# Five turns of the gate and second output projections as seven block products, with the merge stage regrouped

## The reference

```
h = rmsnorm(x)
z = h @ w_in                     # q, k, v, the gates ga and gm, ...
a_out = forgetting_attention(...)        # 256 x 1024
m_out = rmsnorm(mlstm(...)) * sigmoid(...)   # 256 x 1024
merged = sigmoid(ga) * (a_out @ w_proj_a) + sigmoid(gm) * (m_out @ w_proj_m)
x = x + merged @ w_out           # 2048 x 2048
h2 = rmsnorm(x)
u = causal_conv(h2 @ w_up); x = x + (silu(u_gate) * u_val) @ w_down
```

## Time and profile before

| | us |
|---|---|
| median of 3 runs (2109.66 to 2109.86) | 2109.82 |
| the profiled execution's own time | 2109.87 |
| its span in the trace | 2108.1 |
| PE busy in the span | 2102.6 (100%) |
| DVE busy | 1432.9 (68%) |
| ACT busy | 1092.6 (52%) |
| POOL busy | 17.5 (1%) |

### The profile page before, as it was taken

One profiled execution on the slowest core, in us unless ns is written; L12 is line 12 of the kernel. 1 busy time (PEld: TensorE's weight loads), 2 busy tenths in 40 slices (PEclk: granted clock), 3 DMA queues, 4 the chain that ended last, 5 costly groups with the idle time before them and its releaser, 6 DMA issues.

```text
span 2108.1 us, 25121 instructions
## 1 busy us (share of the span) xinstructions
PE 2102.6 (100%) x10042; PEld 1759.9 (83%) x10042; DVE 1432.9 (68%) x1605; ACT 1092.6 (52%) x1292; POOL 17.5 (1%) x17
## 2 busy tenths in 40 slices
PE   9999999999999999999999999999999999999999
PEld 8888888888888887887888888888888888888887
DVE  7987556655787754655654555567777777779986
ACT  6765444444456544544444444555555555555553
POOL 0000000000000000000000000000000000000000
PEclk9999999999999999999999999999999999999999
DMA  8665555555764554544455555556555555556653
GB/s 335 209 203 176 192 192 188 192 186 180 270 224 154 196 195 168 169 158 149 143 193 194 190 189 190 181 171 198 190 180 198 189 183 192 188 171 236 224 203 134
DMA packets 111956, 404.39 MB, mean 192 GB/s; under 512 B 12512, under 2 KB 13280, under 8 KB 111328
## 3 DMA queue, kind: packets, MB, share of 16 engines
q1 hardware_dynamic: 109440, 394.66, 55.6%
q10 hardware_dynamic: 2400, 8.14, 1.0%
HBM read 400.65 MB, written 2.10 MB: 191 GB/s over the span
## 4 chain that ended last, share of the span: by engine, by line
PE 97%; DVE 2%; DMA 1%; ACT 1%; issue 0%; ACTq 0%; DVEq 0%
PE g L529 45%; PE g L620 17%; PE xs L548 8%; PE g L548 8%; PE xs L643 4%; PE xs L552 4%; PE g L552 4%; PE g L647 3%; PE xs L571 1%; DVE w_lo L1330 1%; PE xs L799 1%; PE xs L680 1%; DMA raw<-in_stream 0%; PE xs L796 0%; ACT w_hi L940 0%; DMA xf<-in_x 0%
## 5 line engine op out<-in xcount | busy, mean ns | idle before, releaser
L1330 DVE TENSOR_TENSOR w_lo<-raw,w_hi 128x1024 fp32r<-128x1024 f32 x679 | 828.2, 1223 | 593.2 <-ACT w_hi L940 589.1
L940 ACT ACTIVATE w_hi<-raw 128x1024 fp32r<-128x1024 f32 x679 | 718.9, 1059 | 823.5 <-PE g L529 519.2
L529 PE MATMUL g<-w_hi,mid_both 128*128 128x512 f32 x1280 | 406.7, 393 | 0.0
L529 PE MATMUL g<-w_hi,in_both 128*128 128x512 f32 x1024 | 318.7, 390 | 0.1
L529 PEld LDWEIGHTS g<-w_hi,mid_both 128*128 128x128 f32 x1280 | 240.3, 188 | 49.4
L529 PE MATMUL g<-w_lo,mid_both 128*128 128x512 f32 x640 | 249.1, 389 | 0.0
L529 PEld LDWEIGHTS g<-w_hi,in_both 128*128 128x128 f32 x1024 | 192.3, 188 | 40.1 <-DVE v_all L1459 0.5
L529 PE MATMUL g<-w_lo,in_both 128*128 128x512 f32 x512 | 199.2, 389 | 0.0
L548 PE MATMUL g<-mlp_both,w_hi 128*128 128x512 f32 x704 | 176.7, 393 | 0.4 <-DVE xw L1782 0.4
L548 PE MATMUL xs<-mlp_both,w_hi 128*128 128x512 f32 x704 | 176.3, 392 | 0.0
L548 PEld LDWEIGHTS g<-mlp_both,w_hi 128*128 128x128 f32 x704 | 126.6, 189 | 23.5 <-DVE xw L1782 0.8
(11 more groups left out here) (346 smaller groups left out, 2716.8 us busy)
## 6 DMA issues: line engine op xcount, KB each, us to landing
raw<-in_stream SPq DMA_DIRECT2D x679, 512.0 KB, 3.3
d_block<-in_stream SPq DMA_DIRECT2D x28, 512.0 KB, 4.4
v_block<-in_stream SPq DMA_DIRECT2D x20, 512.0 KB, 4.5
o_block<-in_stream SPq DMA_DIRECT2D x16, 512.0 KB, 4.8
x_first<-in_x_tokens ACTq DMA_DIRECT2D x2, 1024.0 KB, 6.6
gain_row<-in_gain_rows SPq DMA_DIRECT2D x8, 256.0 KB, 3.5
xt<-in_x_tokens ACTq DMA_DIRECT2D x1, 2048.0 KB, 8.0
xf<-in_x SPq DMA_DIRECT2D x3, 512.0 KB, 8.4
```

Source lines behind the costliest of these rows:

```text
L529: ins = mm(G[buf][:, t, :], a[:, kt, at_t], w[:, slot, j * COLS:(j + 1) * COLS], start=(kt == 0 and n == 0), stop=(last and j == ROWS_PER_ ...
L940: activation(w_hi[:, n % RING, :], of[:], ACT.Copy).then_inc(hi_ready, 1)
L1330: v.tensor_tensor(w_lo[:, n % RING, :], of, w_hi[:, n % RING, :].bitcast(F32), ALU.subtract).then_inc(lo_ready, 1)
```

## The change

The merge stage becomes two rounds of a pair of column blocks: the m gate of 1024 columns as a wide group (`gm0`, `gm1`), then both a projections (`pa`), then both m projections (`pm`). In `gm0` all four turns go in two `MIXED` steps, two of them by products; in `gm1` one of four turns is by products; `out2` becomes two wide groups, one of whose four turns each is by products. That is five turns by products. `gm1` and `out2` use a new order, `MIXED_LATE`, in which a plain chunk comes first. `merged_turned` is placed after item 1 of the next stage for blocks 1 and 3, and after item 6 of `pm` for blocks 0 and 2. `x_turned(4)` and `(5)` come after items 0 and 2 of the second group of `out2`, `(6)` and `(7)` after chunks 0 and 2 of `up`.

```diff
-    ("merge", [8, 4, 4] * 4),
+    ("gm0", [8] * 2), ("pa0", [4] * 2), ("pm0", [4] * 2),
+    ("gm1", [8] * 2), ("pa1", [4] * 2), ("pm1", [4] * 2),
...
+    "gm0": (((0, 3), (1, 2)),),
+    "gm1": (((0, None), (1, 3), (2, None)),),
+    "out2": (((0, None), (2, 1), (3, None)),) * 2,
...
+SUMS_AT = {"v": (4, 8), "out1": (1, 4), "down": (3, 6, 9, 64), "gm0": (-8, -5), "out2": (-7,)}
...
 MIXED = (1, "C0", 5, 7, "C1", 6, 3, "C2", 4, 2, "C3")
+MIXED_LATE = ("C0", 1, "C1", 5, 7, "C2", 6, 3, "C3", 4, 2)
...
+             FIRST_ITEM["gm0"] - 4: ("gm0", B11), FIRST_ITEM["gm0"] - 3: ("gm0", B12),
+             FIRST_ITEM["gm0"] - 2: ("gm0", B22), FIRST_ITEM["gm0"] - 1: ("gm0", B21),
...
```

PE: where it transposes, and what it waits for (`merged_turned` and the loops):

```diff
             def merged_turned(i):
                 pe.wait_ge(sem["merged_ready"], i + 1)
+                if i % 2 == 0:
+                    pe.wait_ge(sem["own_read"], own_ahead(f"gm{i // 2}") + 1)
...
+                for n in range(items_of(gm)):
...
+                        if item.product == 1 and p == 1:
+
+                            pe.wait_ge(sem["merged_lo_ready"], 2)
...
+                    if p and n == 1:
+                        merged_turned(1)
...
+                    if n == 6:
+                        merged_turned(2 * p)
+
+            out2_second = items_of("out2") // 2
+            for n in range(items_of("out2")):
...
+                    if item.product == 1 and item.group == 1:
+
+                        pe.wait_ge(sem["g_lo_ready"], 6)
...
+                if n == 1:
                     merged_turned(3)
-                if c >= 8 and c % 8 == 1:
-                    x_turned(4 + c // 8 - 1, xw[:, :, col_block(c // 8 - 1)])
+                if n == out2_second:
+                    x_turned(4, xw[:, :, col_block(0)])
+                if n == out2_second + 2:
+                    x_turned(5, xw[:, :, col_block(1)])
 
             for c in range(176):
...
-                if c == 1:
+                if c == 0:
+                    x_turned(6, xw[:, :, col_block(2)])
+                if c == 2:
                     x_turned(7, xw[:, :, col_block(3)])
```

DVE:

```diff
+            def gate_m_result(gm, h):
+
+                dve.wait_ge(mm_done, half_end(gm, 0, h) + 1)
+                by_t = ((gm_wide.p1, gm_wide.u_b), (gm_wide.u_a, gm_wide.u_d))[h]
+                for t in range(2):
+                    ins = v.tensor_tensor(gate_m[h][:, t, :], GG[:, 2 * h + t, :], by_t[t][:], ALU.add)
+                ins.then_inc(group_read[h], 1)
...
+                for n in range(8):
+                    split(pm, n)
...
+                    if n == 4:
+                        m_projected(p, 0)
...
+                    if n == 7:
+                        merged_low(2 * p)
+                        m_projected(p, 1)
...
+            for n in range(items_of("out2")):
...
+                split("out2", n)
+                if n == 2:
                     merged_low(3)
-                if c >= 8 and c % 8 == 2:
-                    gained_low(norm_mlp, c // 8 - 1, 4, TR)
+                add_products("out2", at_item, xw)
+                if n in (out2_second + 1, out2_second + 3):
+                    gained_low(norm_mlp, (n - out2_second) // 2, 4, TR)
...
-                    if i == 0 and k == 2:
-                        gained_low(norm_mlp, 3, 4, TR)
-                    if i == 0 and k == 3:
+                    if i == 0 and k in (1, 3):
+                        gained_low(norm_mlp, 2 + k // 2, 4, TR)
+                    if i == 0 and k == 4:
                         dve.wait_ge(sem["sq_ready"], 12)
```

More of the change, by code:

```diff
@@ L108 @@
         for _turn, _by_products in _steps:
-            for _what in (PLAIN if _by_products is None else MIXED):
+            for _what in (PLAIN if _by_products is None else MIXED_LATE if _name in ("gm1", "out2") else MIXED):
                 if _what in PLAIN:
@@ L177, in sum_slot @@
 def sum_slot(phase, turn):
-    return SUM_TURNS[phase].index(turn)
+    return SUM_TURNS["gm0" if phase == "gm1" else phase].index(turn)
 def sums_ahead(phase):
@@ L379, in build @@
                      ("y", 88 * kib))
-    wide = {"v": v_wide, "out1": out1_wide, "down": down_wide}
+    wide = {"v": v_wide, "out1": out1_wide, "gm0": gm_wide, "gm1": gm_wide, "out2": out2_wide, "down": down_wide}
     u_sum = sb("u_sum", "mix", 4 * kib, [P, 4, S])
@@ L488, in _ @@
                         sp.wait_ge(sem["f_lo_ready"], UP_TURNS)
+                    if phase == "gm0":
+                        sp.wait_ge(sem["am_lo_ready"], 4)
+                    if phase == "out2" and b in (B22, B21):
+                        sp.wait_ge(group_read[1], group_of("pa1", 1)[2])
                     if phase == "out1" and b in (B11, B12):
@@ L882, in _ @@
[L882 to L884 removed]
+                blocks_turned(gate_a[i % 2]).then_inc(sem["merged_turned"], 1)
+            for p in range(2):
+                gm, pa, pm = f"gm{p}", f"pa{p}", f"pm{p}"
+                for n in range(items_of(gm)):
+                    at_item = FIRST_ITEM[gm] + n
+                    item = ITEMS[at_item]
+                    pe.wait_ge(lo_ready, at_item + 1)
+                    if item.product:
+                        if item.product == 1 and p == 0:
+                            pe.wait_ge(sem["m_done"], M_HEADS)
+                            pe.wait_ge(sem["sums_lo_ready"], sums_ahead("gm0") + sum_slot("gm0", item.turn) + 1)
+                        if item.product == 1 and p == 1:
+                            pe.wait_ge(sem["merged_lo_ready"], 2)
+                        ins = wide_product(item, norm_mid.hi, norm_mid.lo, at_item % RING)
+                    else:
+                        ins = wide_chunk(item, norm_mid.hi, norm_mid.lo, at_item % RING)
+                    ins.then_inc(mm_done, 1)
+                    if p and n == 1:
+                        merged_turned(1)
+                for n in range(8):
+                    one(pa, n // 4, n % 4, tokens(pa, n // 4, am_hi[:, 0:8, :], am_lo[:, 0:8, :],
+                                                  None if n >= 4 or p else "am_lo_ready"))
+                for n in range(8):
+                    one(pm, n // 4, n % 4, tokens(pm, n // 4, am_hi[:, 8:16, :], am_lo[:, 8:16, :],
+                                                  None if n >= 4 or p else "am_lo_ready", 2))
+                    if n == 6:
+                        merged_turned(2 * p)
@@ new lines, in _ @@
+            out2_second = items_of("out2") // 2
+            for n in range(items_of("out2")):
+                at_item = FIRST_ITEM["out2"] + n
+                item = ITEMS[at_item]
+                pe.wait_ge(lo_ready, at_item + 1)
+                if item.product:
+                    if item.product == 1 and item.group == 0:
+                        pe.wait_ge(sem["merged_lo_ready"], 4)
+                        pe.wait_ge(sem["sums_lo_ready"], sums_ahead("out2") + 1)
+                    if item.product == 1 and item.group == 1:
+                        pe.wait_ge(sem["g_lo_ready"], 6)
+                    ins = wide_product(item, g_hi, g_lo, at_item % RING)
+                else:
+                    if item.group == 0 and item.half == 0 and item.row % 2 == 0:
+                        pe.wait_ge(sem["merged_lo_ready"], item.turn + 1)
+                    ins = wide_chunk(item, g_hi, g_lo, at_item % RING)
+                ins.then_inc(mm_done, 1)
+                if n == 1:
@@ L1016, in first_product @@
                             act.wait_ge(sem["sq_ready"], 4)
+                        elif phase == "gm0":
+                            act.wait_ge(sem["m_done"], M_HEADS)
+                        elif phase == "gm1":
+                            act.wait_ge(sem["merged_turned"], 2)
+                        elif phase == "out2" and g == 0:
+                            act.wait_ge(mm_done, FIRST_ITEM["out2"])
+                        elif phase == "out2":
+                            act.wait_ge(sem["own_read"], own_ahead(phase, g))
                         elif phase == "v":
@@ L1753, in _ @@
                         "am_hi_ready", q + 1, "am_lo_ready")
+                sums_low("gm0", c - 96)
+                sums_of_rows("gm0", c - 96, norm_mid.hi, norm_mid.lo)
             def merged_low(i):
@@ new lines, in _ @@
+            for p in range(2):
+                gm, pa, pm = f"gm{p}", f"pa{p}", f"pm{p}"
+                for n in range(items_of(gm)):
+                    at_item = FIRST_ITEM[gm] + n
+                    last_of_own_products(gm, at_item)
+                    for h in range(2):
+                        if at_item == half_end(gm, 0, h):
+                            gate_m_result(gm, h)
+                    split(gm, n)
+                    if p and n == 2:
+                        merged_low(1)
+                    own_products(gm, at_item)
+                for n in range(8):
+                    split(pa, n)
+                    if n == 4:
+                        a_projected(p, 0)
+                for n in range(8):
+                    split(pm, n)
```

(14 more changed lines are left out.)

154 lines of the change are left out of this document (80 added, 74 removed).

## The result

| | before | with the change |
|---|---|---|
| median, us | 2109.72 (2109.61 to 2109.86, 10 runs) | 2115.30 (2113.51 to 2116.26, 10 runs) |
| profiled execution, us | 2109.87 | 2113.51 |
| span in the trace, us | 2108.1 | 2111.7 |
| mean granted clock | 1.000 | 0.999 to 0.998 |

The ratio is 1.0025, with a 95% interval of 1.0015 to 1.0035. The change makes the kernel slower by some 5.6 us, 0.26%; that it is slower is clear, that it is past the bound of 0.2% is not, since the interval begins at 0.15%. The time also scatters: before, ten runs lie within 0.25 us (the 27 and 30 runs beside the later experiments within 1.2 and 0.7); now within 2.75. They fall into two sets that go with the clock: three runs at 0.999 take 2113.5 to 2114.0 us, seven at 0.998 take 2115.2 to 2116.3.

The account below looks back on a forecast made before the run. PE, almost never waiting, was taken to bound the kernel. Fewer matmuls and new waits, -6.80 + 1.52 + 5.54 + 1.45 + 0.34 = +2.05 us on 2109.87, gave 2111.9 us, range 2108.5 to 2115.5.

Parts of the forecast that it names:

- rival 3: DVE becomes the bound in the gate stage, from product 7 of `gm0`'s first step: 2114.4 us, slower; chance 12%.
- rival 4: The clock falls to half for two chunks behind each of two 2.8 us waits: 2122.8 us; chance 4%.
- The gain: Five turns by products save 30 matmuls on PE at 226.7 ns each: 6.80 us less.
- (d): End of `gm0`: the first chunk of `pa0` waits for the bank that product 2 ends, 0.3 us.
- (a): At `merged_turned(1)` and `(3)`, PE waits because a `merged_low` now stands ahead of the sum: 0.76 us twice, 1.5 us.
- (b): In `out2`, `x_turned(5)` and the second group's first product each wait 2.77 us for `gained_low`; together 5.5 us.
- T+5.49: In `out2`, XS comes free for PE 5.49 us after the end of the item ahead; PE arrives after 2.72.
- (c): At `x_turned(7)` in `up`, PE waits for `gained_low` behind a plain split, with one chunk of cover: 1.45 us.
- The sum: The saved matmuls and all new waits of PE added up: +2.05 us, giving 2111.9 us.
- Work beside PE at 0 in `gm0`: DVE's extra work hides beside PE in `gm0`; at product 7 it just fits, 0.4 us to spare: cost 0.
- The clock at 0: PE's granted clock stays full in the changed kernel, so the forecast time holds no cost for it.

Follow-up runs that it names:

- The best version: Changed kernel with the four `gained_low` steps of `out2` and `up`, and `merged_low` of blocks 0 and 2, ahead of their splits: 2103.28 us.
- the run with the filler: Changed kernel with seven extra matmuls of ones, their result never read, ahead of each of the two long waits in `out2`: 2112.41 us.

## Why the prediction was right, and where it was wrong

Forecast 2111.9 us and "the same"; measured 2115.3, inside the range of 2108.5 to 2115.5, but slower by 0.26%, and to more than 0.2% I gave 16%. The waits came as forecast. That the time still lies inside the range, by 0.2 us, is luck: the upper end was set a us above rival 3, which did not happen, and the range left out rival 4, which did, at about a quarter of the price that I gave it. Point by point:

- *The gain, 6.80 us.* Right: 30 matmuls less, and one turn undone costs 1.34 of the 1.36 counted. The best version shows it nearly whole: 6.46 us under the kernel before, for 6.80 less the 0.3 of (d). The Trainium skill's gap of about 216 ns for an isolated matmul of 512 columns (TensorE: Matmul & The Clock Gate, Back-to-back issue gap) would make a turn 1.30 us, by estimate. The medians can't tell that from 1.36, but the traces' 1.36 and their 226.7 ns can.
- *(a), 0.76 each.* Right: DVE's rows follow each other as counted, and the end of the sum releases PE.

```profile
1289.19 1.22 DVE L1858 SCALAR_TENSOR_TENSOR g_lo<-xs,g_hi 128x1024 fp32r<-128x1024 f32 x1
1290.32 1.21 DVE L1880 SCALAR_TENSOR_TENSOR gate_m<-gate_m,g 128x1024 f32<-128x1024 f32 x1
1291.57 1.22 DVE L1882 TENSOR_TENSOR gate_a<-gate_a,gate_m 128x1024 f32<-128x1024 f32 x1
...
1292.85 1.09 PE L597 MATMUL xs<-ident,gate_a 128*128 128x128 f32 x8 [0.55 <-DVE gate_a L1882]
```

  The gap between matmuls is 0.94 us for 0.23 (1291.91 to 1292.85), 0.71 lost, and 0.07 more goes in the restart: with the low parts earlier it is 138.47 us from the first transposes of `gate_a` (1194.96) to those of `xw` (1333.43), against 136.90 with both waits gone, 1.57 for the two. The medians differ by 1.67, for 1.52 counted. The bracket's 0.55 is less than what it costs, since a matmul's record runs 0.39 us while the stream moves on every 0.23.
- *(b), 2.77 each.* Right in place and nearly in size; in the trace the gaps are 3.17 and 3.01 us for 0.23, 2.9 and 2.8 lost. (The T+5.49 holds 0.1 for PE's release, as (c) has it: 4.14 + 1.25 is 5.39. And the cover before was seven items, not eight: chunks 11 to 17 of `out2` stood between `gained_low` of block 0 and `x_turned(5)`.)
- *(c), 1.45.* Right: the low parts end at 1392.92, PE starts 0.15 later after 1.34 idle. (b) and (c) together are the 7.46 us between the run with the filler and the one with all low parts earlier (6.99 counted).

```profile
1391.27 1.65 DVE L1474 SCALAR_TENSOR_TENSOR mlp_both<-xs,par,mlp_both 128x256 fp32r<-128x256 f32 x4
...
1393.07 1.06 PE L597 MATMUL xs<-ident,xw 128*128 128x128 f32 x8 [1.34 <-DVE mlp_both L1474]
```

- *(d), 0.3.* Right: ahead of the first matmul of `pa0` its weight load waits on `gate_m`, and the gap between matmuls is 0.48 for 0.23, 0.25 us. (The sum has 0.34 where 93.32 - 92.99 is 0.33.)
- *Work beside PE at 0 in `gm0`.* Right, with 0.33 us to spare where I counted 0.4. Rival 3 did not happen; the run with one more operation shows that it stood one operation away.
- *The clock at 0.* This step failed. Rival 4 happened, to which I gave 4% "since nothing in this trace shows a drop". That trace had no idle stretch beyond 0.4 us once started, so it could not speak on the question. The Trainium skill did (TensorE: Matmul & The Clock Gate, HAM oscillation — how this bites in real kernels): it has the clock fall after idle gaps between bursts of matmuls, in an example with gaps of some 3 to 5 us. The changed trace agrees that it falls after such a gap, 0.61 of the clock granted in the 3.5 us behind the first long wait, and here 2.8 us without work was enough in some executions. I named the section in rival 4 and kept the 4% all the same. The two waits start 10.6 us apart (1339.35 and 1349.96 are the last matmuls ahead), not 9. The price was smaller than I gave the rival, 2.9 us for 10.9: I had PE at half clock for two chunks behind each wait, and in the trace it was at full clock again after eight transposes and about three matmuls; in that of the kernel with `x_turned(5)`'s wait alone before the first chunk behind them was done.

Without the clock the sum comes to 2112.4 by the filler's run, 0.5 above the forecast: most of it in (b) and (c) (7.46 for 6.99).

## What to carry to other kernels

On a bound engine that runs in order, count for each wait that you move how many items of cover it keeps: of the two costly waits here the first had seven items before and one after, and the second was new, with one. The step that released each stood behind two operations that nobody was waiting for yet. Put what PE waits for ahead of the work that only fills a ring; that alone turned +5.6 us into -6.5 here. Take an idle stretch of TensorE like these of 2.8 us as dearer than its length (those of 1.4 us were not), and look at mean clock and scatter of the runs for it, since the page's clock row can look full.

## What was not expected of the hardware

- An idle stretch of 2.8 us lowered TensorE's clock in 9 of 20 executions with one such stretch, at a cost of some 1.5 us each; three stretches of 1.4 us did so in none of 10, and stretches of 1.1 to 1.3 us in none of 11.
- With both stretches of 2.8 us in one kernel the clock fell in all ten executions, more often than two separate chances would give.
- The clock did not always fall within the idle stretch. In one trace it was full through the stretch and nearly all of the eight transposes behind it.
- Seven fp32 matmuls of 128 columns into the same bank took 1.72 us right behind other matmuls (14 records), 0.25 us each, where the filler had been sized at 0.39 from the start of the kernel (17 of them in 6.71 us).
- The record of PE's idle time understates a wait by about 0.16 us, for the last matmul's record outlasts its place in the stream.
